# Six products with V moved in the slot tables of a two-block transformer kernel

## The reference, cut to what matters

```python
scores = jnp.einsum('bnqkgd,bnmkd->bkgnqm', qb, kw).astype(jnp.float32)
logits = jnp.where(valid, scores + bias, NEG_INF)
...
probs = jnp.exp(logits - lse[..., None])
out = jnp.einsum('bkgnqm,bnmkd->bnqkgd', probs.astype(v.dtype), vw)
```

```python
hid = jax.nn.gelu(jnp.einsum('bnlgd,ldf->bngf', blocks, w1))
return jnp.einsum('bngf,fd->bngd', hid, w2)
```

## Time and profile before

| | |
|---|---|
| time, median of 3 runs | 1158.64 us (1157.67 to 1159.46) |
| the profiled execution: its time, its span | 1158.94 us, 1157.1 us |
| PE busy | 1141.3 us, 99% of the span |
| PEld, DVE, ACT, POOL busy | 950.2, 823.7, 586.4, 137.2 us |
| granted TensorE clock | 0.996 of full speed |
| HBM | 189 GB/s over the span |

### The profile page before, as it was taken

How to read it: one execution, slowest core, us unless ns; L and a number is a source line. 1 busy time by engine, 2 the same in 40 slices (tenths; PEclk the granted TensorE clock), 3 DMA queues, 4 the chain that set the end, 5 groups by cost and what they waited for, 6 DMA issues and landing times.

```text
span 1157.1 us, 15957 instructions
## 1 busy us (share of the span) xinstructions
PE 1141.3 (99%) x6207; PEld 950.2 (82%) x6207; DVE 823.7 (71%) x1245; ACT 586.4 (51%) x736; POOL 137.2 (12%) x152
## 2 busy tenths in 40 slices
PE   7999999999999999999999999999999999999997
PEld 6888777787998777878888888998777878888886
DVE  5565656666689899787777454599899787777443
ACT  6445565644436666633555333525776534555332
POOL 1222231100003143000000000003234000000000
PEclk9999999999999999999999999999999999999999
DMA  9545543457545668654555555545677654655640
GB/s 362 193 171 206 194 186 121 175 185 275 171 153 201 208 182 223 195 183 163 184 190 197 212 188 188 177 152 216 187 213 220 182 182 146 218 183 186 217 161 37
DMA packets 35323, 219.34 MB, mean 190 GB/s; under 512 B 3888, under 2 KB 5680, under 8 KB 10928
## 3 DMA queue, kind: packets, MB, share of 16 engines
q1 hardware_dynamic: 32800, 204.67, 50.6%
q0 software_dynamic: 1728, 12.58, 5.8%
q10 hardware_dynamic: 720, 1.06, 0.3%
HBM read 217.25 MB, written 1.05 MB: 189 GB/s over the span
## 4 chain that ended last, share of the span: by engine, by line
PE 81%; issue 15%; DVE 1%; ACT 1%; DVEq 1%; DMA 1%; POOL 0%; POOLq 0%; ACTq 0%
PE panel L921 35%; PE panel L925 17%; PE panel L992 5%; PE tile L1006 4%; PE panel L995 3%; PE panel L969 3%; PE panel L968 3%; PE panel L967 3%; PE heads_out L1346 1%; PE heads_out L1200 1%; PE tile L1260 1%; PE tile L1369 1%; PE tile L1366 1%; DMA area<-in_x_columns_dram 1%; DVEq L2058 1%
## 5 line engine op out<-in xcount | busy, mean ns | idle before, releaser
L630 DVE TENSOR_TENSOR ring_parts<-ring,ring_parts 128x2048 fp32r<-128x2048 f32 (+2 forms) x172 | 389.8, 2271 | 161.5 <-ACT ring_parts L596 155.6
L596 ACT ACTIVATE ring_parts<-ring 128x2048 fp32r<-128x2048 f32 (+2 forms) x184 | 346.8, 1888 | 255.1 <-PE panel L925 203.8
L921 PE MATMUL panel<-ring_parts,hT 128*128 128x512 f32 (+2 forms) x1344 | 329.2, 392 | 4.0 <-issue 2.7
L921 PEld LDWEIGHTS panel<-ring_parts,hT 128*128 128x128 f32 x1344 | 241.2, 189 | 60.3 <-issue 12.7
L921 PE MATMUL panel<-ring_parts,area_parts 128*128 128x512 f32 x736 | 178.5, 391 | 0.0
L925 PE MATMUL panel<-ring_parts,hT 128*128 128x512 f32 (+2 forms) x672 | 170.4, 388 | 0.0
L921 PEld LDWEIGHTS panel<-ring_parts,area_parts 128*128 128x128 f32 x736 | 138.1, 188 | 29.5
L925 PEld LDWEIGHTS panel<-ring_parts,hT 128*128 128x128 f32 x672 | 121.2, 188 | 25.5 <-issue 2.5
L992 PE MATMUL panel<-hT,ring_parts 128*128 128x512 f32 x512 | 129.9, 393 | 0.0
L2205 DVE SCALAR_TENSOR_TENSOR area<-area,cw 128x256 f32<-128x256 f32 x240 | 104.7, 497 | 2.9
L992 PEld LDWEIGHTS panel<-hT,ring_parts 128*128 128x128 f32 x512 | 91.6, 189 | 16.0
(11 more groups left out here) (248 smaller groups left out, 1133.0 us busy)
## 6 DMA issues: line engine op xcount, KB each, us to landing
ring<-in_w_layers_dram SPq DMA_DIRECT2D x140, 1024.0 KB, 4.9
ring<-in_w_first_dram SPq DMA_DIRECT2D x38, 1024.0 KB, 5.0
ring_parts<-in_w_layers_dram POOLq DMA_DIRECT2D x12, 1024.0 KB, 8.7
ring<-in_w_first_dram SPq DMA_DIRECT2D x5, 512.0 KB, 10.1
area<-in_second_bias_dram SPq DMA_DIRECT2D x8, 320.0 KB, 3.2
ring<-in_w_layers_dram SPq DMA_DIRECT2D x4, 560.0 KB, 4.0
area<-in_first_bias_dram SPq DMA_DIRECT2D x4, 384.0 KB, 4.4
area<-in_later_bias_dram SPq DMA_DIRECT2D x1, 1536.0 KB, 12.2
```

Of the source, the lines that this page charges most:

```text
L596: act.activation(ring_lo[:, SLOTS + hi, 0:w], ring[:, slot, 0:w], ACT.Copy).then_inc(high_ready, 1)
L630: g.tensor_tensor(ring_lo[:, slot, 0:w], ring[:, slot, 0:w], ring_lo[:, SLOTS + hi, 0:w], ALU.subtract).then_inc(low_ready, 1)
L921: pe.matmul(ps[:, b, 0:width], t[:, 4 * i + k, b * P:(b + 1) * P], hi[:, k, :], start=(i == k == 0 and t is of[0]), stop=False)
```

## The change

Six numbers of two tables change. In the first block V of pair 1 goes from slot 14 to slot 12 (where S of pair 3 is), and V of pair 2 from 16 to 17 (group 1 of S of pair 4). In each of the two layers V of pair 1 goes from 15 to 14 (cmpFv), V of pair 2 from 22 to 21 (R2), V of pair 4 from 40 to 36 (S of pair 6) and V of pair 5 from 43 to 44 (S of pair 7). No S, E, N or T moves.

```diff
-FIRST_V = (7, 14, 16, 23, 27, 39, 41, 50)
+FIRST_V = (7, 12, 17, 23, 27, 39, 41, 50)
...
-LAYER_V = (8, 15, 22, 29, 40, 43, 51, 55)
+LAYER_V = (8, 14, 21, 29, 36, 44, 51, 55)
```

## The result

| | before | after |
|---|---|---|
| time, median of 20 runs each | 1158.68 us (1157.46 to 1160.15) | 1160.12 us (1159.54 to 1161.72) |
| ratio | | 1.0017, 95% interval 1.0011 to 1.0023 |
| the profiled execution: time, span | 1158.94, 1157.1 | 1161.57, 1159.8 |
| PE, DVE busy | 1141.3, 823.7 | 1141.7, 822.6 |

The changed kernel is slower. The ratio is estimated from all runs, not from the two medians: it says 0.17%, 2.0 us, while the medians are 1.4 us apart. The forecast was 1158.8, no change, and its range ended at 1160.4.

What follows compares the result with a forecast made beforehand. PE's matmul stream was taken to bound the kernel, with DVE nearly full. -0.23 (first block) - 0.01 + 0.36 (layers) = +0.12 us on the profiled 1158.94, which is 0.30 above the median, gave 1158.8 us; range 1156.7 to 1160.4.

Steps and rivals of the forecast that it cites:

- the sum: Whole kernel: -0.23 in the first block, -0.01 in the first layer, +0.36 in the second, together +0.12 us.
- the fold's delay: Each layer: with V of pair 1 ahead of it, the fold comes one V, 0.80 us, later.
- 0.23 a move: PE: V placed directly ahead of another small group saves its two borders, 0.23 us, the seam being free.
- rival 3: The seam beside V costs as much as a border, so 0.115 us a move: 1157.5 us; chance 0.05.
- First block, V of pair 1, counted at nothing: PE's 0.09 us gain is waited away at pair 4's scores, held by ACT's L1552; bounds -0.1 and +1.02.
- The fold's delay reaches cmpS: Each layer: the delay passes through DVE and ACT to PE, which leaves cmpS 0.45 us late; bounds -0.23 and +0.80.
- V of pairs 2, 4 and 5, 0.69 a layer: Each saves PE 0.23 us, as DVE does not wait for the groups behind them; PE reaches cz at -0.24.
- Given back at cz: End of each layer: DVE, 0.45 us late, lets PE leave no earlier than -0.01 (first layer) and +0.36 (second).
- rival 4: Between cmpS and cz, POOL work stretches a DVE instruction by up to 1.41 us a layer: 1161.6 us; chance 0.10, half mild.
- Rival 1: DVE keeps up and the full gain of 2.16 us arrives: 1156.5 us; chance 0.10.

Runs made afterwards that it cites:

- e13_all: The change plus the edits of e12_room, one DVE tap moved behind the logits of pair 7, and cz at slot 63 instead of 62; 1157.37 us, ratio 0.9989.
- e4_behind: The change with V of pair 1 back at its old slot in the first block and directly behind the fold in the layers; 1157.24 us, ratio 0.9994.
- e3_scores: The kernel before with only V of pair 1 of the first block moved, ahead of the scores of pair 3; 1158.06 us, ratio 0.9998.
- e12_room: The change with a DVE tap moved into the wait for the fold and ACT's exps of pair 2 ahead of the gelu; 1157.60 us, ratio 0.9995.
- e11_wait: The kernel before, no V moved, with one DVE tap put ahead of the logits of pair 3 instead of behind; 1162.82 us, ratio 1.0040.
- e2_fold: The kernel before with only V of pair 1 of each layer moved, ahead of the fold; 1160.41 us, ratio 1.0018.
- e8_light: The kernel before with V of pair 1 of a layer at slot 19 instead of 15, lengthening the row of small matmuls; 1158.09 us, ratio 1.0000.
- e1_later: The change with V of pair 1 left where it was before, in the first block and the layers; 1158.08 us, ratio 0.9997.
- e5_cmps: The change with cmpS and R0 of each layer at slot 20 instead of 19, behind six more panel matmuls; 1160.57 us, ratio 1.0021.

## Why the prediction was wrong

Point by point, by its steps. The forecast was no change and the kernel became slower. The step that failed is what the sum did with the fold's delay: it priced the new wait at cmpS at its own length and had no term for TensorE's clock, whose fall makes 1.58 of the 2.0 us between the sum (+0.12) and the traces (+2.1).

- **0.23 a move.** Right in the layers: 0.25 in e13_all, 0.26 and 0.27 for V behind the fold in e4_behind. The seam between V and the group beside it is free within some hundredths, and rival 3 is out.
- **First block, V of pair 1, counted at nothing.** The gain was waited away at L1130, as said, but the scores' delay also passed on in part: +0.27 in the change, +0.24 in e3_scores, inside the bounds of -0.1 and +1.02. L1950 took 0.23 and no longer 1.41, but it started only when POOL's L719 had ended: it ended 0.23 later than before, counted from the first V, where the prediction had let its end stay, and that is what ACT's L1552 handed on to PE. With V of pair 2 the block gives +0.05 where the sum had -0.23.
- **The fold's delay reaches cmpS.** Right in mechanism and nearly in size: +0.34 and +0.35 against +0.45. The logits of pair 3 were 0.42 later, and 0.07 of the 0.22 counted as handover was slack, since with a real wait PE starts 0.15 after L2273 ends. The step that failed is what the sum did with it. It priced the wait at its own length. The wait of 0.4 us was followed by a fall of the clock, 1.58 us in the profiled first layer, a term that the sum did not have at all. e12_room (no wait, no fall, with the change's order of PE) and e11_wait (wait and fall, with the order of before) show both directions of it.
- **V of pairs 2, 4 and 5, 0.69 a layer.** Right, 0.65 at the scores of pair 7 in both layers.
- **Given back at cz.** The cause was right (DVE inherits the delay and none of the gain), the place was wrong. I had looked for slack only where the trace ends the stage. The transposes of pair 6 had less: before, PE started the six at 454.35 and ran them without a pause, though L2273 ended only at 454.51. In the second layer this took 0.93 in the change (the wait of 0.66 and the broken row of transposes around it), where the sum gave back 0.60 at cz. DVE did inherit the delay of cmpS: less the layer's offset of 1.98, L2319 is 0.41 late, and the logits still are at 852 us. At 869 it is 0.58, at the logits of pair 7 0.63. What added this is rival 4's coincidence in a small form. At 864 us one tap of the convolution (L2205) took 1.70 us beside POOL's L740, where before another tap took 1.54 beside it: 0.17. At 881 L2370 took 1.28 instead of 0.23 beside the next L740, and the L2374 behind it 1.15 instead of 2.15: 0.05.
- **The range.** The sum was +0.12 and the result +1.4 by the medians, +2.0 by the ratio, +2.1 by the traces; that the median still lies inside the range is owed to its width, made for other reasons. No rival had the clock; rival 4 came to 2.8 by another way. Rival 1, the full gain of 2.16, is nearly what the moves give (1.9) once three handovers have room.

## What to carry to other kernels

A table edit that takes a few tenths from the engine that bounds the kernel pays only if every handover from a second full engine has slack for it. List all of them between the edit and the end of the stage, with the end of the releasing instruction and the start of the released one, and not only the last. Where a group moves later by one step, follow its readers until they come back to PE. If they bring a new wait of even 0.4 us in front of a long row of small matmuls (here 24, 2.7 us), price not the wait alone but, as a risk, panels at half speed behind it, and read the granted clock there. The cheap cure is room (a tap moved into idle time, a group six matmuls later), and it is worth next to nothing where nobody waits.

## What the hardware showed that was not expected

- The clock fell behind a short wait, although PE shows no idle time in the windows of the fall. It went to 0.50 for about 3 us behind waits of 0.38 to 0.52 us at cmpS, in one of the two layers of each profiled execution that had such waits (after, e2_fold, e11_wait), at a cost of 1.6 us. What makes it the one layer or the other stays open. In the profiled executions without that wait it was 1.00 there in both layers, with the longer row of e8_light too.
- Not each wait does it, and its length does not decide. At the transposes of pair 6, with only six panel matmuls to the next transposes, e1_later waited 0.75 us and the clock stayed at 1.00 from 454 to 464. e5_cmps waited 1.4 us twice ahead of the scores of pair 4 and kept 1.00. Which part of what stands behind the wait at cmpS matters, no run here separates.
- A DVE instruction of 0.41 us took 1.71 when a POOL one of 1.47 started 0.02 ahead of it; in the change one of 0.23 took 1.28. Which instructions meet can change though neither engine's list does: the lists of DVE and POOL were the same in e5_cmps and in the change.
- In each of thirteen waits of 0.35 to 0.77 us for DVE's read of a PSUM tile (after, e1_later, e2_fold, e4_behind, e11_wait, e12_room) PE started 0.15 to 0.16 us after the end of L2273, whatever the length of the wait.
